# Nine ring entries for the gathered expert rows instead of eight, and the first normalisation's vectors loaded per group

## Time and profile before

| what | value |
| --- | --- |
| median of 3 runs | 3387.93 us (3379.59 to 3388.46) |
| profiled execution | 3388.89 us, its span 3387.0 us |
| PE, DVE, ACT, POOL busy | 76%, 67%, 51%, 32% of the span |
| bytes moved | 1219 MB, 1074 MB of them by the gathers |
| mean rate | 360 GB/s over the span, 421 GB/s in the last group |
| POOL waiting for PE to free an entry of `rows` | 1611.3 us |
| DVE waiting for a gathered row in `rows` | 520.3 us |

### The profile page before, as it was taken

How to read it: one execution, slowest core, us unless ns; L and a number is a source line. 1 busy time by engine, 2 the same in 40 slices (tenths; PEclk the granted TensorE clock), 3 DMA queues, 4 the chain that set the end, 5 groups by cost and what they waited for, 6 DMA issues and landing times.

```text
span 3387.0 us, 40375 instructions
## 1 busy us (share of the span) xinstructions
PE 2560.7 (76%) x14180; PEld 2098.1 (62%) x14180; DVE 2260.2 (67%) x5430; ACT 1728.5 (51%) x2282; POOL 1074.0 (32%) x1039
## 2 busy tenths in 40 slices
PE   7989987687888775787987766787897765555655
PEld 4467766566766665666866665666766665555554
DVE  5253067887566778887656777887656787667654
ACT  2111035576555455775645455776545555555544
POOL 1000013334234333443333333433334343333331
PEclk9999998888998996988998997988998987777777
DMA  5122469899999999999999999999999999999997
GB/s 198 54 72 78 149 248 419 332 371 389 386 412 397 420 412 410 388 398 367 412 384 420 419 411 412 390 397 367 419 391 420 419 409 421 421 421 421 421 421 299
DMA packets 194302, 1219.23 MB, mean 360 GB/s; under 512 B 21490, under 2 KB 30707, under 8 KB 62644
## 3 DMA queue, kind: packets, MB, share of 16 engines
q0 software_dynamic: 147456, 1073.81, 77.6%
q1 hardware_dynamic: 34980, 118.92, 9.5%
q10 hardware_dynamic: 11664, 23.92, 1.9%
HBM read 1204.25 MB, written 12.32 MB: 359 GB/s over the span
## 4 chain that ended last, share of the span: by engine, by line
DMA 38%; issue 19%; PE 15%; DVE 13%; ACT 8%; DVEq 6%; POOL 1%; SPq 0%; POOLq 0%
DMA rows<-in_peer_uv,ids_peer 30%; PE acc L748 6%; DVE rows L1066 5%; ACT rows L1325 4%; DMA KT<-in_peer_uv,ids_peer 3%; PE fA L616 2%; DMA hT_g<-hT_spill 2%; DMA V<-in_peer_uv,ids_peer 2%; PE mB L673 2%; ACT L1317 1%; PE fA L639 1%; DVEq L926 1%; ACT S L1259 1%; PE fB L639 1%; DVE S L935 1%
## 5 line engine op out<-in xcount | busy, mean ns | idle before, releaser
L398 POOL DMA_INDIRECT rows<-in_peer_uv,ids_peer x916 | 954.6, 1042 | 1981.6 <-PE acc L748 1611.3
L748 PE MATMUL acc<-ident,rows 128*128 128x128 f32 x7328 | 1117.3, 308 | 565.4 <-ACT rows L1325 553.7
L1325 ACT ACTIVATE rows<-rows,coef 128x1024 f32<-128x1024 f32 x916 | 1015.2, 1142 | 830.3 <-DVE coef L1077 830.2
L748 PEld LDWEIGHTS acc<-ident,rows 128*128 128x128 f32 x7328 | 963.6, 160 | 735.6 <-ACT rows L1325 672.5
L1066 DVE CUSTOM_DVE_ANT_0 rows<-rows,hh 128x1024 f32<-128x1024 f32 x486 | 590.4, 1221 | 263.0 <-DMA rows<-in_peer_uv,ids_peer 257.4
L1066 DVE CUSTOM_DVE_ANT_0 rows<-rows,fB 128x1024 f32<-128x1024 f32 x430 | 522.1, 1216 | 266.9 <-DMA rows<-in_peer_uv,ids_peer 263.0
L616 PE MATMUL fA<-hT_g,wring 128*128 128x256 f32 x1024 | 238.4, 388 | 26.4 <-DMA hT_g<-hT_spill 26.4
L673 PE MATMUL mB<-hT_g,wring 128*128 128x256 f32 x1024 | 248.7, 399 | 1.1 <-ACT hT_g L1288 1.1
L616 PEld LDWEIGHTS fA<-hT_g,wring 128*128 128x128 f32 x1024 | 196.1, 196 | 53.1 <-DMA hT_g<-hT_spill 27.1
L673 PEld LDWEIGHTS mB<-hT_g,wring 128*128 128x128 f32 x1024 | 203.0, 204 | 29.4 <-ACT hT_g L1288 1.4
L1317 ACT ACTIVATE act_out<-dots 128x2 f32<-128x2 f32 x512 | 102.5, 200 | 224.6 <-DVE dots L1066 222.7
(11 more groups left out here) (215 smaller groups left out, 2779.4 us busy)
## 6 DMA issues: line engine op xcount, KB each, us to landing
wring<-in_wstream SPq DMA_DIRECT2D x192, 512.0 KB, 7.8
rows<-in_peer_uv,ids_peer POOLq DMA_INDIRECT x916, 11.3
hT_spill<-rows ACTq DMA_DIRECT2D x1, 4096.0 KB, 11.7
wring<-in_wstream SPq DMA_DIRECT2D x16, 256.0 KB, 7.1
hT_g<-hT_spill ACTq DMA_DIRECT2D x4, 1024.0 KB, 25.7
out_h<-hh ACTq DMA_DIRECT2D x8, 512.0 KB, 9.3
S<-in_w_lat SPq DMA_DIRECT2D x1, 2048.0 KB, 12.7
hT_g<-in_x SPq DMA_DIRECT2D x4, 512.0 KB, 4.0
```

The costliest lines, as they stand in the source:

```text
L398: pool.indirect_dma_start(both(g, i), None, peer_uv, bass.IndirectOffsetOnAxis(ap=ids_peer[:, t, s:s + 1], axis=0)).then_inc(row_in[entry( ...
L748: last = mm(acc[:, tok(k)], v_row(g, i)[:, tok(k)], ident[:, :], is_transpose=True, start=i % SLOTS == 0 and k % 4 == 0, stop=i % SLOTS == ...
L1325: s.activation(row, row, ACT.Copy, scale=coef[:, b, i % BATCH:i % BATCH + 1]).then_inc(scaled, 1)
```

## The change

`NE` becomes 9 (and with it `NL` 15). The 8 KB per partition for the new entry come from `ln`, which shrinks from four vectors to two and keeps those of the second normalisation alone. For the first group, gamma and beta of the first normalisation lie in rows 14 and 15 of `rows` (entry 7), which are free until the gathers begin. For each later group ACT loads them again, at step 129, into the upper half of `S2`, which the second tile's lists have left by then; for that the lists are closer together, so that the last ends at step 126 instead of 138. A new semaphore tells ACT that the last list has been read, another tells DVE that the vectors have landed.

```diff
-NE = 8
+NE = 9
-R_LISTS = [spread(a, 3, 3) for a in (8, 26, 44, 62, 80, 98, 116, 132)]
+R_LISTS = [spread(a, 3, 3) for a in (8, 24, 40, 56, 72, 88, 104, 120)]
+LN1_LOAD = 129
-        ln = sb("ln", [P, 4, D])
+        ln = sb("ln", [P, 2, D])
+        ln1_first = rows[:, KD + 6:KD + 8, :]
+        ln1_again = S2[:, 1, :, :].rearrange("p c n -> p (c n)").rearrange("p (j d) -> p j d", j=2)
-        dft_sb = ln[:, 2:4, :]
+        dft_sb = ln[:, :, :]
-        w_uk_sb = ln[:, 0, :].rearrange("p (k n) -> p k n", k=2)
-        w_uv_sb = ln[:, 1, :].rearrange("p (k n) -> p k n", k=2)
+        w_uk_sb = rows[:, KD + 6, :].rearrange("p (k n) -> p k n", k=2)
+        w_uv_sb = rows[:, KD + 7, :].rearrange("p (k n) -> p k n", k=2)
...
         def entry(g, i):
-            return i % NL if g == GROUPS - 1 else (g * STEPS + i) % NE
+            if g == GROUPS - 1:
+                r = i % NL
+                return r if r >= NE else (g * STEPS + r) % NE
+            return (g * STEPS + i) % NE
...
# DVE, first normalisation
                             if g == 0:
                                 dve.wait_ge(hres_in, 16)
+                            else:
+                                dve.wait_ge(ln1_in, 32 * g)
...
+                        ln1 = ln1_again if g > 0 else ln1_first
                         normalise(1, h1_front[:, t, :], h1_front[:, t, :], std1, g * TILES + t + 1,
-                                  ln[:, 0, :], ln[:, 1, :], h1_done)
+                                  ln1[:, 0, :], ln1[:, 1, :], h1_done)
...
# DVE, lists of the second tile
-                        topk(cand, cv[:, t, h, :], ci[:, t, h, :])
+                        last = topk(cand, cv[:, t, h, :], ci[:, t, h, :])
+                        if t == 1 and h == PH - 1:
+                            last.then_inc(lists_read, 1)
...
# ACT, front
+                if m == LN1_LOAD and g > 0:
+                    act.wait_ge(lists_read, g)
+                    for j in range(2):
+                        act.dma_start(ln1_again[:, j, :], lnp[3 + j:4 + j, :].to_broadcast([P, D])).then_inc(ln1_in, 16)
```

More of the change, by code:

```diff
@@ L88 @@
 assert FIRST_LISTS[0][2] < FIRST_ALONE[0] and FIRST_ALONE[3] < US0 and BATCH < AHEAD < NE and VS0 + LEAD <= STEPS
+assert R_LISTS[PH - 1][2] < LN1_LOAD < L0
 assert FIRST_LISTS[PH - 1][2] < STEPS + A0 + 7 and FIRST_IDS[PAIRS - 2][3] < STEPS
@@ L253, in layer_program @@
         gates_sb, m_done = sem("gates_sb"), sem("m_done")
+        lists_read, ln1_in = sem("lists_read"), sem("ln1_in")
         var1, std1, h1_done, h1T_ps, h1T_sb = (
@@ L302, in landed @@
                 return row_in[entry(g, i)], 16 * ((g * STEPS + i) // NE + 1)
-            before = g * STEPS // NE if entry(g, i) < NE else 0
+            before = (g * STEPS + i % NL) // NE if i % NL < NE else 0
             return row_in[entry(g, i)], 16 * (before + i // NL + 1)
@@ L906, in topk @@
                 dve.drain()
-                v.max_index(idx16[:, 8:16], val16[:, 8:16], vals)
+                return v.max_index(idx16[:, 8:16], val16[:, 8:16], vals)
             def front(g, m):
@@ L1087, in finish_norm @@
             def finish_norm(g, t):
-                normalise(2, h1_peer[:, t, :], h1_peer[:, t, :], std2, g * TILES + t + 1, ln[:, 2, :], ln[:, 3, :],
+                normalise(2, h1_peer[:, t, :], h1_peer[:, t, :], std2, g * TILES + t + 1, ln[:, 0, :], ln[:, 1, :],
                           out_ready)
@@ L1368, in dft @@
                     for j in range(4):
-                        act.dma_start(ln[:, j, :], lnp[3 + j:4 + j, :].to_broadcast([P, D])).then_inc(ln_in, 16)
+                        dst = ln1_first[:, j, :] if j < 2 else ln[:, j - 2, :]
+                        act.dma_start(dst, lnp[3 + j:4 + j, :].to_broadcast([P, D])).then_inc(ln_in, 16)
                     for i in range(2):
```

## The result

The changed kernel took 3356.49 us (median of five runs, 3355.58 to 3356.74); the kernel before, in alternation with it, 3383.82 us (3374.05 to 3388.46). The ratio is 0.9919, 95% interval 0.9905 to 0.9932: faster by some 27 us, where 14 had been forecast. The profiled execution has a span of 3353.6 us, before 3387.0. One of the six executions of the changed kernel in a later series took 8283.61 us and is left out of that series' median.

The account below looks back on a forecast made before the run. DMA transfers bound most stages (417 to 421 GB/s), with holes in attention and at steps 85 and 133 where the ring ran short; -7.5 - 7.5 - 7.5 - 2 + 7.5 + 3 = -14.0 gave 3374.9 us, range 3358 to 3392.

Parts of the forecast that it names:

- the base: Whole kernel: the profiled execution of the kernel before, 3388.89 us, from which the forecast's terms were subtracted.
- ring, attention: Attention, three loops: the ninth entry gives one gather per loop, -7.5 us (bounds 0 and -34).
- ring, step 85: PE's wait for `hT_g`, three times: one more gather runs inside POOL's 16.0 us pause, -7.5 us (from below 0).
- lists onto steps 71 to 77: Attention: a moved head falls on the expert numbers and DVE starts late, +3 us (bounds 0 and +19).
- ring, step 133: Step 133, three times: one more gather fits the hole of 7.0 us, -7.5 us (0 to -7.5).
- last lists earlier: Steps 126 to 129: ACT's wait for the last list before loading the vectors costs 0.
- vectors loaded again: From step 129, three times: two 512 KB broadcasts, charged as full transfer time, +7.5 us (from below 0).
- loop ends: End of each loop, 3.4 us lost there: the ninth entry gives -2 us in all (0 to -10).
- The rule that was weighed: Step 85: a deeper gather queue would slow `hT_g` where that queue ran empty; judged not so, 7.5 us at stake.
- The last group: Last group, ring of 15 instead of 14: already at 421 GB/s, nothing to win, 0.
- the hole that only moves: Rival: step 133's saving pays for the vectors, attention gives nothing, step 85 perhaps 7.5; about 3385 us, chance 0.31.
- the lists' collision: Rival, steps 71 to 78: DVE too late, transfers stop, head's 6.4 us show per loop (+19); 3400.4 us, chance 0.14.

Follow-up runs that it names:

- ring alone: Changed kernel's nine entries and reloaded vectors (load at step 140), lists at their old steps: 3378.41 us against 3388.54 for the kernel before, ratio 0.9969.
- head back: Changed kernel with one head of the lists moved from step 72 to 79: 3368.37 us against 3387.84 for the kernel before, ratio 0.9946.
- no reload: Changed kernel without the vector loads; later groups' first normalisation reads the second's vectors: 3346.71 us against 3388.54 for the kernel before, ratio 0.9875.
- lists alone: Kernel before, eight entries and resident vectors, with only the lists at the new steps: 3379.5 us against 3388.54, ratio 0.9975.
- late heads: Kernel before with only the last two heads moved, from 116 and 132 to 114 and 121: 3376.6 us against 3383.76, ratio 0.9978.
- larger pieces: Changed kernel with the spill laid out by groups, 128 pieces of 8 KB per load: 3357.62 us against 3383.76 for the kernel before, ratio 0.9924.
- wider heads: Changed kernel with the spill laid out by groups and lists at 8, 22, 43, 59, 79, 93, 114, 121: 3359.69 us against 3383.76 for the kernel before.
- PE's broadcast: Changed kernel with the vectors spread by PE products and copied by ACT instead of reloaded: 3357.26 us against 3383.6 for the kernel before, ratio 0.9919.
- larger pieces, before: Kernel before with the spill laid out by groups, 128 pieces of 8 KB per load instead of 1024 of 1 KB: 3378.7 us against 3383.76, ratio 0.9982.
- one head: Kernel before, eight entries, with only the head at step 80 moved to 72: 3392.82 us against 3388.54, ratio 1.0018.

## Why the prediction was right in direction and half as large as the gain

Its places were right: the rate rose where it had been low, and the bytes of the reload were paid. Two readings were off without weight for the sum: the DMA engines are at 80 to 90 per cent from the seventh slice on, not the sixth, and the base, 3388.9, lies 5.1 us above the median of before. So 5.1 of the 18.4 us between 3374.9 and 3356.5 are the base, and 13.3 the gain. Term by term, forecast beside measured (loops, us):

```
term                          forecast   measured
ring, attention                 -7.5       -9.3   (ring alone, 0-88)
ring, step 85                   -7.5       -1.3   (ring alone, 88-104)
lists onto steps 71 to 77       +3        -10.1   (after less head back: 48-88 +12.3, 88-104 -22.4)
ring, step 133                  -7.5       -4.0   (104-160, no reload less lists alone)
last lists earlier               0        -11.9   (104-160, lists alone; the same in late heads)
vectors loaded again            +7.5       +9.6   (after less no reload)
loop ends                       -2         -1.1
```

The measured column has differences from different neighbours and adds to -28.1; the loops lost 31.8, so 3.7 us are not assigned. The term of the loop ends lies within what one kernel's repeat moves (3.4).

- *"the pause of 16.0 us exceeds 11.3 + 2.49 = 13.8, so the new gather runs whole inside the hole"*: this step failed. The depth that it read off, about 4.5 gathers, was near the 4.0 to 4.3 counted; but it took for granted that an added entry is an added gather in flight. With nine entries 4.2 to 4.5 were in flight at that point in the ring alone, and 3.7 to 4.1 with the head put back. The ninth lay as a landed row before DVE in the one and as a dotted row before PE in the other, and steps 88 to 104 gave 1.3 us of 7.5. What holds the queue at four gathers there is not shown. Over the whole kernel the ninth entry does stand in the queue: a gather's median landing went from 11.3 to 13.8 us, one gather more.
- *"I charge 1 us per loop for the cases where it starts late, +3"*: the collision came as described and cost more, 12.3 us by the head put back, inside the bounds of 0 to 19. This step failed by what it left out, what the collision brings: while DVE is late the gather queue stays low, `hT_g` lands in 12.6 us instead of 25.7, and PE's wait of 26.4 us goes. I had the two numbers side by side, the landing beside a full queue and a cover that runs dry, and asked only what the deeper queue would do to `hT_g`, not what the moved lists would do to the queue.
- The rule that was weighed, the Trainium skill (DMA: Bandwidth & Descriptors, Queues, rings and completion order), by which the queues take turns by packets, fits what was measured, and it was the way to the cause: beside gathers the landing fell from 25.7 to 12.6 us where their queue stayed low, and to 9.7 where `hT_g`'s pieces were as large as theirs. The conclusion "by this landing the gain stays" was drawn for the wrong edit.
- Step 133: the prediction laid the hole to the ring. PE's wait there comes from the head at 132, which the change moves to 120. The prediction priced the move of the last head only as ACT's wait for the last list, 0. The ring's own share (-4.0) is worked out beside the new lists; with the old ones the ring alone, reload included, moves 104 to 160 by +1.0, so about -8.6 if the reload costs 9.6 there too. No run had nine entries, the old lists and no reload; this share stays between the two.
- Attention and the vectors: the sizes were 2 us off each. For the vectors the mechanism is shown, by the kernel that leaves their loads out; for attention only the size is, and it depends on the lists (0 to 88 falls by 17.4 with the head put back).
- The last group gave nothing, as forecast: 535.8 against 535.6 us.
- Of the rivals, the hole that only moves describes the ring alone at step 85; the lists' collision describes the single head with eight entries, which is the one kernel that was slower. Neither describes the whole, in which ring and lists seem to help each other: 0.31 and 0.25 per cent alone, 0.81 together. The lists open the way for `hT_g`, and the longer ring, probably with the wider spacing, keeps attention from paying for it.

Among versions that do all the work none beat the changed kernel by more than can be measured: larger pieces, wider heads and PE's broadcast end at the same time. The larger pieces found no wait left; the other two gave back in the next stage what they had gained.

## What to carry to other kernels

Before a ring entry is counted as depth of the DMA queue, see how many entries are in flight and how many are rows that have landed and wait for a reader or for their release; here a ninth entry left the queue at the pause at four gathers. A load that shares the engines with a deep queue landed here more by its number of pieces than by its bytes, so lay it out in pieces as large as its rival's, or have it issued where that queue is short (here by a moved list; moving the load itself was not tried), and check every moved step for which of these it changes. When an engine is late before one stage and idle behind it, price both sides in one sum: the lateness cost 12 us here and freed 22.

## What the runs showed of the hardware

That the landing of 1 MB could vary so much with nothing but its neighbour and its layout was not expected. Beside a full gather queue it took 24.8 to 26.6 us in pieces of 1 KB (the kernel before) and 9.0 to 10.7 in pieces of 8 KB (larger pieces, before). In pieces of 1 KB beside a queue that stays low it took 8.0 to 16.1 (changed kernel, lists alone, one head). With no gathers at all, in the first group, it took 6.1 in pieces of 1 KB and 4.9 in pieces of 8 KB, so the small pieces are slow only in company.

In the packed trace of before a piece of 8 KB took 320 ns on its engine and one of 1 KB 51. While the 1024 pieces of one load were under way there, 994 to 1121 pieces of gathers were moved, and 1291 to 1462 of the load's own queue, with the first of the load behind it: not far from one for one. With turns piece by piece, 1024 pieces on 16 engines are 64 rounds of 0.371 us, 23.7 us, which is near what was seen. The 128 pieces of 8 KB are 8 rounds of 0.640, 5.1 us; seen were 9.0 to 10.7. Some 2.3 us of that are there without a neighbour too (4.9 us, of which its own pieces make 8 x 0.320 = 2.6); the rest is open. That is an estimate from these numbers; it fits equal numbers of pieces per turn, and the runs do not tell whether a turn is one piece or several.
